# Scan rotation tables built on GpSimd during the second expert loop, window copies on VectorE, small mixing loads in SyncE's queue

## The chip, the cores and the metric

The kernel runs on one core of a Trainium2 chip. The metric is the device time of one execution in microseconds. The core's engines are TensorE (PE in the profile; its weight loads are PEld), VectorE (DVE), ScalarE (ACT), GpSimd (POOL) and SyncE (SP). Each runs its own list of instructions in order and meets the others only through semaphores. DMAs are issued from SyncE's and ScalarE's queues here and are carried by 16 DMA engines.

## The reference

One sequence of 256 tokens of 1024 channels goes through two blocks. The first block has two layers; the first mixes by pooling and the second by latent attention, and each ends with a mixture of 32 experts, of which every token uses two. The second block has one layer: a mixing layer, cross attention over a memory of 256 tokens, and a convolutional feed-forward part. All values are float32.

The part that the change touches most is the state-space branch (`_s5`) of the mixing layer. It has 32 groups of 64 complex states, each driven by 16 channels:

```
lam = lam_re + i*lam_im                    # per group and state
dt = exp(log_dt)                           # per group
a_bar = exp(lam * dt)
b_bar = (a_bar - 1) / lam * b
bu[t] = b_bar @ u[t]
s[t] = a_bar * s[t-1] + bu[t]              # complex, over 256 tokens
y[t] = real(c @ s[t]) + d * u[t]
```

`a_bar`, `b_bar` and the powers of the rotation `exp(i*th)`, th = lam_im*dt, depend on weights alone and on no token.

## The kernel before

**Stages.** The work runs in the order: pooling layer, experts of layer 0 (`moe(0)`), latent attention (`mla`), experts of layer 1 (`moe(1)`), mixing layer (`mix`), `cross`, `ffn`. Big weights come as slabs of 2 MB (4096 floats in each of 128 partitions) into a ring of six. SyncE issues them in one order, each when the slab six places before it has been used (`slabs_done`); so the loads of a later stage begin while an earlier one still computes. An expert takes three slabs (gate, up, down).

**The arena.** Nearly all other buffers are fixed places in one tile called `arena`, handed from stage to stage. `xs` holds the tokens sorted by expert; `hT` is the transposed input of a layer and is free during an expert loop, and `XN`, the normalised input, is free once the sorting products have read it.

**Pooling layer.** ScalarE (from L1261) normalises x, issues the four router loads of layer 0 (`router_loads`, L1233 to L1237), and writes the upper half of the transposed blocks (`hT_upper`, L1257) into `pl`; VectorE writes the lower half. TensorE multiplies them by `pool_w` (L640), beginning with the lower half. GpSimd scales the bias (L2138) and adds it to x (L2142). VectorE then adds TensorE's products to x (L1596, L1597: eight instructions), which frees layer 0's experts: TensorE transposes x (L612) and computes the router's logits (L655).

**Expert loop.** Before it, every token is routed and sorted; at its start, VectorE and ScalarE scale the sorted blocks (ScalarE at L1298). For each expert GpSimd reads the expert's first slot from memory into a register (`value_load`) and copies its window of 64 tokens out of `xs` into one of two `xw` buffers (L2165). TensorE multiplies the window by gate and up (L729), ScalarE applies silu (L1318), VectorE multiplies by the up part (`hids`, L1702), TensorE transposes (L745), ScalarE copies (L1325), TensorE multiplies by down (L772) and combines the experts' outputs with gate columns (L758) that VectorE makes one expert ahead of use (`window_gates`, L1714 and L1717). The steps are written with TensorE's gate and up products of the next expert ahead of the down product of the present one. A register loop runs over the experts between the first two and the last two.

**Mixing layer.** ScalarE issued twelve small loads during the routing of layer 1 (`s5_loads`): the state weights `s5_rows` and `ldt2`, `b_in`, four parts of `c_rows`, the input-gate weights `w_if` and their biases. The gain of the final norm of block one was issued in the expert loop (L1307). After the loop x is normalised twice. TensorE transposes the state rows (L971) and `c_rows` (L975) and computes the first slab, `u`. VectorE meanwhile computes the discretised states on tiles of 128x16 (L1870 to L1916): dt, the reduced angle `th`, `a_bar`, `b_bar` (`bbar`) and the powers `wre`, `wim` of the rotation for 1, 2, 4, ... 128 tokens.

The scan has eight steps q, each of four groups (two columns of 128 states). TensorE: one slab of the layer's input projection (L950 or L961), transposes of the padded b (L1057), the outputs of step q-1 (`outputs`, L996), the state inputs of step q (L1066), and for q from 3 a part of the other branch, the mLSTM (`gates_between`: L1005, L1011, L1019, L1028, L1035). GpSimd: masks b (`bpad`, L2205), builds the table of the rotation's 256 powers for the step's two columns by doubling, in eight levels of six instructions (L2216 to L2221), the four products of a level waiting for the level before, and masks c (`cblk`, L2229). VectorE: rotates the inputs with the table (L1994 to L2000), scans (L2004), rotates back (L2007 to L2014, `states`), and between the steps does convolutions (L1849, L1854), the skip term (L1928) and the mLSTM's exponents (L1947 to L1959) and products. ScalarE: evacuates slabs, copies the transposed b (L1454), and applies exponentials (L1485 to L1489) and gates (L1465). ScalarE's copy for step 5 stands behind the exponentials, which wait for VectorE's exponents of step 4.

The wait that ties VectorE to GpSimd in each step is this:

```
dve.wait_ge(s["e_ready"], q + 1)
dve.wait_ge(s["bu_mm"], q + 1)

dve.tensor_tensor(r1, u_re, e_re, ALU.mult)
```

## Time and profile before

| | |
|---|---|
| median of 3 runs | 1870.59 us (1866.02 to 1873.18) |
| profiled execution, its own time | 1867.0 us |
| its span in the profile | 1865.2 us |
| TensorE busy | 1657.4 us (89%) |
| VectorE busy | 447.4 us (24%) |
| ScalarE busy | 234.1 us (13%) |
| GpSimd busy | 234.7 us (13%) |
| DMA, mean over the span | 270 GB/s; 504 MB in all |
| TensorE's mean granted clock | 0.958 of full speed |

The profile shows one execution. A timeline row has the start and the duration in microseconds, the engine, the line, the operation, what it writes and reads, and in brackets how long the engine was idle before it and what ended that. A share of busy time is a mean over stages with different limits, so the stages have to be read one by one. Stages by time: pooling layer to 31 us, routing of layer 0 to 65, first expert loop to about 535, attention to 678, routing of layer 1 to 712, second expert loop to 1179, mixing layer to about 1430, the rest to the end.

### The profile page before, as it was taken

To read this page: it belongs to the slowest core of one execution; us is meant where nothing else is said; L and a number is where in the kernel's file an instruction comes from. 1 tells how busy PE (TensorE), PEld (TensorE's weight loads), DVE (VectorE), ACT (ScalarE), POOL (GpSimd) and SP (SyncE) were. 2 spreads that over 40 slices of the span, in tenths; PEclk is the share of its full clock that TensorE was granted. 3 is DMA by queue.
4 is the path that set the end of the run, shared out by engine and by line. 5 is a ranking of instruction groups with operands and counts; after the bars stand their busy time and mean duration, and the time that the engine had idled before them with its cause. 6 is when DMAs were issued, how large, how long until landed. Compare 5 with 4: busy or idle time off the path is not lost.

```text
span 1865.2 us, 22408 instructions
## 1 busy us (share of the span) xinstructions
PE 1657.4 (89%) x8961; PEld 1036.5 (56%) x8961; DVE 447.4 (24%) x964; ACT 234.1 (13%) x504; POOL 234.7 (13%) x495
## 2 busy tenths in 40 slices
PE   5899989999988678999989899798788898899998
PEld 4655444444446546554444444576677585488853
DVE  3211111111122231111111111475563102133411
ACT  2010000000021311000000000312111111100000
POOL 1000000000000000000000000099960000000000
PEclk8899999999998788999999999999899898999999
DMA  9499999999994035999999999832223343344410
GB/s 345 187 396 426 425 426 427 427 426 426 426 347 181 0 109 204 426 427 427 426 426 425 426 427 424 330 104 75 83 91 132 116 143 128 102 136 136 156 47 23
DMA packets 104421, 504.29 MB, mean 270 GB/s; under 512 B 16714, under 2 KB 42667, under 8 KB 71595
## 3 DMA queue, kind: packets, MB, share of 16 engines
q1 hardware_dynamic: 90551, 497.21, 66.0%
q10 hardware_dynamic: 13812, 6.31, 1.2%
q8 instruction: 37, 0.61, 0.1%
q14 instruction: 21, 0.17, 0.0%
HBM read 502.45 MB, written 1.05 MB: 270 GB/s over the span
## 4 chain that ended last, share of the span: by engine, by line
PE 50%; DMA 32%; POOL 9%; DVE 4%; issue 3%; ACT 2%; POOLq 0%; SPq 0%; DVEq 0%; ACTq 0%
DMA ring<-in_w_up 32%; PE PS L729 12%; PE PS L1183 8%; PE PS L1193 4%; PE PS L1130 3%; PE PS L961 3%; PE PS L772 3%; PE PS L674 2%; PE PS L1120 2%; PE PS L935 1%; PE PS L1111 1%; POOL arena L2220 1%; POOL XN L2219 1%; POOL XN L2216 1%; POOL arena L2221 1%
## 5 line engine op out<-in xcount | busy, mean ns | idle before, releaser
L729 PE MATMUL PS<-ring,arena 128*64 128x256 f32 x4096 | 470.1, 384 | 76.3 <-DMA ring<-in_w_up 53.5
L729 PEld LDWEIGHTS PS<-ring,arena 128*64 128x64 f32 x4096 | 296.7, 138 | 271.5 <-DMA ring<-in_w_up 73.9
L772 PE MATMUL PS<-ring,arena 128*64 128x512 f32 x1024 | 233.8, 598 | 1.1 <-ACT arena L1325 1.1
L1702 DVE TENSOR_TENSOR arena<-PS,arena 128x256 f32<-128x256 f32 x64 | 27.2, 425 | 802.5 <-ACT arena L1318 802.5
L2165 POOL COPY arena<-arena 128x512 f32 x64 | 60.5, 945 | 856.1 <-DVE arena L1702 796.6
L772 PEld LDWEIGHTS PS<-ring,arena 128*64 128x64 f32 x1024 | 68.2, 136 | 157.7 <-issue 157.7
L1183 PE MATMUL PS<-hT,ring 128*128 128x256 f32 x704 | 153.8, 382 | 1.0 <-issue 1.0
L1183 PEld LDWEIGHTS PS<-hT,ring 128*128 128x128 f32 x704 | 134.8, 192 | 20.0 <-issue 1.3
L758 PE MATMUL PS<-arena 64*128 64x512 f32 x512 | 127.2, 615 | 1.9 <-ACT arena L1334 1.9
L950 PE MATMUL PS<-hT,ring 128*128 128x256 f32 x448 | 100.3, 385 | 0.0
L950 PEld LDWEIGHTS PS<-hT,ring 128*128 128x128 f32 x448 | 86.4, 194 | 12.4 <-issue 0.5
L1325 ACT ACTIVATE arena<-PS 128x256 f32<-128x256 f32 x64 | 24.6, 384 | 521.1 <-PE PS L745 521.1
L1334 ACT ACTIVATE arena<-PS 128x512 f32<-128x512 f32 x64 | 38.2, 597 | 307.5 <-PE PS L772 304.1
L1193 PE MATMUL PS<-ring,arena 128*128 128x512 f32 x176 | 75.7, 592 | 0.0
L758 PEld LDWEIGHTS PS<-arena 64*128 64x128 f32 x512 | 44.1, 186 | 41.5 <-issue 30.2
L1193 PEld LDWEIGHTS PS<-ring,arena 128*128 128x128 f32 x176 | 33.4, 190 | 41.7 <-issue 41.4
L961 PE MATMUL PS<-ring,arena 128*128 128x512 f32 x128 | 55.4, 593 | 1.1 <-ACT arena L1530 1.1
L1849 DVE TENSOR_SCALAR arena<-PS,VT 128x256 f32<-128x256 f32 x52 | 24.9, 538 | 103.7 <-PE PS L1183 95.7
L1714 DVE SCALAR_TENSOR_TENSOR arena<-arena 128x512 f32<-128x512 f32 x64 | 47.5, 743 | 0.2
L1854 DVE SCALAR_TENSOR_TENSOR arena<-PS,VT,arena 128x255 f32<-128x255 f32 (+2 forms) x112 | 46.8, 476 | 1.2
L1717 DVE TENSOR_TENSOR arena<-arena 128x256 f32<-128x256 f32 x64 | 44.2, 691 | 2.2
L674 PE MATMUL PS<-arena,XN 128*128 128x256 f32 x128 | 36.6, 449 | 8.2 <-DVE arena L1666 8.2
(372 smaller groups left out, 1466.4 us busy)
## 6 DMA issues: line engine op xcount, KB each, us to landing
ring<-in_w_gate SPq DMA_DIRECT2D x64, 2048.0 KB, 25.5
ring<-in_w_up SPq DMA_DIRECT2D x64, 2048.0 KB, 25.6
ring<-in_w_down SPq DMA_DIRECT2D x64, 2048.0 KB, 24.6
ring<-in_f_w_up SPq DMA_DIRECT2D x22, 1024.0 KB, 6.6
ring<-in_w_in SPq DMA_DIRECT2D x9, 2048.0 KB, 20.5
ring<-in_f_w_down SPq DMA_DIRECT2D x5, 2048.0 KB, 7.7
ring<-in_x_wkv SPq DMA_DIRECT2D x4, 2048.0 KB, 8.0
ring<-in_wo SPq DMA_DIRECT2D x2, 2048.0 KB, 13.5
```

What stands on the lines that cost most here:

```text
L674: mm = pe.matmul(PS[:, 4 * half + c // 2, c % 2 * T:(c % 2 + 1) * T], XN_rows[:, t, c, :], sel[:, t, half * T:(half + 1) * T], start=(t == ...
L729: mm = pe.matmul(PS[half * WINDOW:(half + 1) * WINDOW, bank, m * half_f:(m + 1) * half_f], xw[bank][:, k, :], mat[:, k, half * half_f:(hal ...
L758: mm = pe.matmul(PS[:, 4 + 2 * t + half, :], buf[rows, t * P:(t + 1) * P], y2[rows, :], start=first, stop=last, skip_group_check=True)
L772: mm = pe.matmul(PS[half * WINDOW:(half + 1) * WINDOW, 3, :], hidT[:, w, k * WINDOW:(k + 1) * WINDOW], mat[:, k, half * 512:(half + 1) * 5 ...
L950: mm = pe.matmul(PS[:, b, f % 2 * T:(f % 2 + 1) * T], w[:, k, f * P:(f + 1) * P], x[:, k, :], start=(k == 0), stop=(k == kx - 1))
L961: mm = pe.matmul(PS[:, bank + t, :], x[:, k, t * P:(t + 1) * P], w[:, k, :], start=(k == 0), stop=(k == kx - 1))
L1130: mm = pe.matmul(PS[:, 2 * half + f // 2, f % 2 * T:(f % 2 + 1) * T], w[:, k, f * P:(f + 1) * P], x[:, k, :], start=(k == 0), stop=(k == K ...
L1183: mm = pe.matmul(PS[:, 2 * (j % 2) + h, f * T:(f + 1) * T], w[:, k, h, f * P:(f + 1) * P], hT[:, k, :], start=(k == 0), stop=(k == KD - 1))
L1193: mm = pe.matmul(PS[:, 4 + 2 * t + half, :], gF[:, c, t * P:(t + 1) * P], w[:, c - 4 * j, half * 512:(half + 1) * 512], start=(c == 0), st ...
L1714: dve.scalar_tensor_tensor(gates2, slots[:, 0, :], slot_of[:, w, bass.ds(linear(e, 1, 0), 1)], slots[:, 1, :], ALU.is_equal, ALU.mult).the ...
L1854: ins = dve.scalar_tensor_tensor(v, ps(f)[:, 0:T - back], taps[f][back], v, ALU.mult, ALU.add)
L2165: pool.tensor_copy(xw[(e[1] * windows + w) % 2], xs[:, :, bass.ds(start + w * WINDOW, WINDOW)])\
```

## The change

- **State matrices.** The three small state loads are issued by SyncE at the program's start. TensorE transposes the state rows in the pooling layer, after both halves of `pl` are written and before the pool products. ScalarE, after its upper blocks, issues the router loads, copies the transposed rows and takes dt; GpSimd, after adding the bias to x, computes what VectorE did before (`s5_discretise`, with the three subtractions of the angle now two instructions each). The reciprocal stays with VectorE, which waits for GpSimd's denominator in front of the pooling layer's output. TensorE waits for dt before it transposes x for layer 0.
- **Tables.** After the sorts of layer 1 GpSimd builds the rotation tables of all eight steps at once (`s5_tables`) into a 32 KB part of the arena (`E`), with `XN` as scratch, and then `bbar`. One signal, `e_ready`, tells that all is there.
- **Window copies.** VectorE makes them in both expert loops, right after `hids` and in front of `window_gates`, two experts ahead.
- **Loads.** `b_in` is loaded by ScalarE in the second expert loop, where the gain was. The gain, `c_rows`, `w_if` and the biases are issued by SyncE ahead of the mixing slabs, behind a wait for the last up slab.
- **Places.** The gate tables `slots`, `gates2` and `gates` move into `hT`, other buffers move within the arena; the gate outputs `gT` lie over `E`, so ScalarE waits for a step's states before it writes them.

```diff
@@ SyncE
+            for at, name in ((0, "s5_lam_re_2"), (32, "s5_lam_im_2")):
+                sp.dma_start(s5_rows[at:at + S5J, :], a[name][0].rearrange("(j g) p -> j (g p)", g=2)).then_inc(s["s5_loaded"], 16)
+            sp.dma_start(ldt2[64:64 + S5J, :], a["s5_log_dt_2"][0].rearrange("(j g) -> j g", g=2)).then_inc(s["s5_loaded"], 16)
             sp.wait_ge(s["vec2_loaded"], 16 * (len(VEC_PARTS) - FIRST_VECTORS))
...
+            def mix_loads():
+                sp.dma_start(gain, a["final_norm"].partition_broadcast(P)).then_inc(s["gain_loaded"], 16)
+                for ri, n in enumerate(("re", "im")):
+                    for d in range(2):
+                        sp.dma_start(c_rows[:, ri, :, d * S5P:(d + 1) * S5P],
+                                     a[f"s5_c_{n}_2"][0].rearrange("(c g) h p -> (g h) c p", c=S5C)).then_inc(s["mix_loaded"], 16)
+                sp.dma_start(w_if, w_in[:, IN_IF:IN_GATE].rearrange("(k p) n -> p k n", p=P)).then_inc(s["mix_loaded"], 16)
+                sp.dma_start(b_if[:, 0:MH], a["m_b_i_2"]).then_inc(s["mix_loaded"], 16)
+                sp.dma_start(b_if[:, MH:], a["m_b_f_2"]).then_inc(s["mix_loaded"], 16)
+            sp.wait_ge(s["slabs_done"], MIX0 - 2)
+            mix_loads()
@@ TensorE, pooling layer
+            pe.wait_ge(s["s5_loaded"], 16 * 3)
+            pe.wait_ge(s["s5_small"], 1)
+            hT_wait("pool")
+            for i in range(3):
+                r = slice(32 * i, 32 * i + S5J)
+                mm = pe.transpose(PS[:, 5 + i, 0:S5J], s5_rows[r, :], ident[r, r])
+            mm.then_inc(s["s5_turned"], 1)
@@ TensorE, moe
                 pe.wait_ge(s["x_ready"], MOE_X[layer])
+                if layer == 0:
+                    pe.wait_ge(s["s5_dt"], 1)
@@ ScalarE, pooling layer
             norm("pool")
-            router_loads(0)
             act.wait_ge(s["vec_ready"], 1)
             hT_upper("pool", ["pool_norm"], dsts=[pl])
+            router_loads(0)
+            act.wait_ge(s["s5_turned"], 1)
+            act.activation(lre, PS[:, 5, 0:S5J], ACT.Copy)
+            act.activation(lim, PS[:, 6, 0:S5J], ACT.Copy)
+            act.activation(dt, PS[:, 7, 0:S5J], ACT.Exp).then_inc(s["s5_dt"], 1)
+            act.wait_ge(s["s5_th"], 1)
+            act.activation(rad, xdt, ACT.Exp)
+            act.activation(sh, th, ACT.Sin, scale=0.5)
+            act.activation(s1, th, ACT.Sin).then_inc(s["s5_sin"], 1)
@@ ScalarE, moe
-                if layer:
-                    s5_loads()
...
-                        act.dma_start(gain, a["final_norm"].partition_broadcast(P)).then_inc(s["gain_loaded"], 16)
+                        s5_b_loads()
@@ ScalarE, mix
                 def gate(i):
                     j = i - MIX_SLABS.index("g0")
+                    act.wait_ge(s["states"], j + 1)
@@ VectorE, pooling layer
             dve.wait_ge(s["pool_biased"], TT)
+            dve.wait_ge(s["s5_th"], 2)
+            dve.reciprocal(den, den).then_inc(s["s5_small"], 1)
             for half in range(2):
@@ VectorE, experts
+                    def window(e, w):
+                        if isinstance(e[0], int) and linear(e, windows, w) == 2:
+                            sorted_wait(1)
+                        if isinstance(e[0], int) and linear(e, 1, 0) >= EXPERTS:
+                            return
+                        start = dve.value_load(starts[0:1, bass.ds(linear(e, 1, 0), 1)], min_val=0, max_val=SLOTS)
+                        dve.tensor_copy(xw[(e[1] * windows + w) % 2], xs[:, :, bass.ds(start + w * WINDOW, WINDOW)])\
+                           .then_inc(g["window"], 1)
...
                                 hids(next_expert(e), w)
+                                window(*after(next_expert(e), w))
                             window_gates(e, w)
@@ VectorE, mix
-                    dve.wait_ge(s["e_ready"], q + 1)
+                    if q == 0:
+                        dve.wait_ge(s["e_ready"], 1)
                     dve.wait_ge(s["bu_mm"], q + 1)
@@ GpSimd
+            def s5_discretise():
+                pool.wait_ge(s["s5_dt"], 1)
+                pool.tensor_tensor(xdt, lre, dt, ALU.mult)
+                step(pool.tensor_tensor(th, lim, dt, ALU.mult))
+                step(pool.tensor_scalar(kq, th, 1.0 / (2 * math.pi), None, ALU.mult))
+                step(pool.tensor_scalar(kq, kq, 12582912.0, None, ALU.add))
+                step(pool.tensor_scalar(kq, kq, 12582912.0, None, ALU.subtract))
+                for part in (6.28125, 0.0019350051879882812, 3.019915981956753e-07):
+                    step(pool.tensor_scalar(ta, kq, part, None, ALU.mult))
+                    step(pool.tensor_tensor(th, th, ta, ALU.subtract))
+                pool.tensor_scalar(th, th, 3.1415925, -3.1415925, ALU.min, ALU.max).then_inc(s["s5_th"], 1)
+                pool.tensor_tensor(ta, lre, lre, ALU.mult)
+                step(pool.tensor_tensor(tb, lim, lim, ALU.mult))
+                pool.tensor_tensor(den, ta, tb, ALU.add).then_inc(s["s5_th"], 1)
...
+            def s5_tables():
+                pool.wait_ge(s["sorted_mm"], KD // 2 * 4)
+                pool.wait_ge(s["slots_spread"], 2)
...
+                for k in range(8):
+                    n = 1 << k
+                    m = min(S5J // 2, 256 // n)
...
+                    for q in range(0, S5J // 2, m):
...
+                        pool.tensor_tensor(tmp[0], e_re[:, :, :, 0:n], g_re, ALU.mult)
+                        pool.tensor_tensor(tmp[1], e_im[:, :, :, 0:n], g_im, ALU.mult)
+                        pool.tensor_tensor(tmp[2], e_re[:, :, :, 0:n], g_im, ALU.mult)
+                        step(pool.tensor_tensor(tmp[3], e_im[:, :, :, 0:n], g_re, ALU.mult))
+                        pool.tensor_tensor(e_re[:, :, :, n:2 * n], tmp[0], tmp[1], ALU.subtract)
+                        step(pool.tensor_tensor(e_im[:, :, :, n:2 * n], tmp[2], tmp[3], ALU.add))
...
+            s5_discretise()
+            moe(0)
+            moe(1)
+            s5_tables()
             mix()
```

## Rows read from the trace of the kernel before

**Rows 1.** The page, the chain that ended last, by engine.
```profile
PE 50%; DMA 32%; POOL 9%; DVE 4%; issue 3%; ACT 2%; POOLq 0%; SPq 0%; DVEq 0%; ACTq 0%
```

**Rows 2.** Windows: stretch, length, busy us (instructions), granted clock, DMA share, GB/s.
```profile
820.00:1170.00 350.00, 317.94 (x2162) 156.45 (x2158) 43.84 (x74) 30.33 (x73) 21.53 (x22) 1.00 1.01 426
1210.00:1400.00 190.00, 166.54 (x699) 132.02 (x699) 116.75 (x206) 36.37 (x56) 163.24 (x420) 0.93 0.26 92
1284.00:1286.00 2.00, 2.00 (x6) 1.64 (x5) 0.00 (x0) 1.01 (x1) 1.82 (x9) 0.50 0.92 371
```

**Rows 3.** Waits in the scan, 1210 to 1390 us.
```profile
DVE XN L1994 <- POOL arena L2221: 39.5, 4, 11.3
```

**Rows 4.** Timeline of VectorE in scan steps 2, 4 and 7.
```profile
1271.32 0.69 DVE L1994 TENSOR_TENSOR XN<-PS,arena 128x512 f32<-128x512 f32 x1 [11.26 <-POOL arena L2221]
...
1316.03 0.69 DVE L1994 TENSOR_TENSOR XN<-PS,arena 128x512 f32<-128x512 f32 x1 [9.57 <-POOL arena L2221]
...
1332.48 1.66 DVE L1959 TENSOR_TENSOR arena<-arena 128x512 f32<-128x512 f32 x2
...
1382.97 0.69 DVE L1994 TENSOR_TENSOR XN<-PS,arena 128x512 f32<-128x512 f32 x1 [8.30 <-POOL arena L2221]
```

**Rows 5.** Timeline of TensorE in scan steps 3 to 5.
```profile
1283.41 3.40 PE L996 MATMUL PS<-arena 128*128 128x256 f32 x8 [4.16 <-DVE arena L1928]
...
1307.97 1.88 PE L1011 MATMUL PS<-arena,const 128*128 128x512 f32 x4
...
1338.84 3.78 PE L1066 MATMUL PS<-arena 128*128 128x256 f32 x8 [7.82 <-ACT arena L1454]
```

**Rows 6.** Timeline of GpSimd, levels 0 and 7 of step 0's table.
```profile
1213.15 0.20 POOL L2219 TENSOR_TENSOR XN<-arena,mtmp 128x2 f32<-128x2 f32 x1
1213.42 0.20 POOL L2220 TENSOR_TENSOR arena<-XN 128x2 f32<-128x2 f32 x1
...
1226.36 0.72 POOL L2221 TENSOR_TENSOR arena<-XN 128x256 f32<-128x256 f32 x1
```

**Rows 7.** Timeline of VectorE and TensorE in the second expert loop.
```profile
1135.55 0.42 DVE L1702 TENSOR_TENSOR arena<-PS,arena 128x256 f32<-128x256 f32 x1 [12.99 <-ACT arena L1318]
...
1136.66 0.72 DVE L1717 TENSOR_TENSOR arena<-arena 128x256 f32<-128x256 f32 x1
...
1140.49 3.67 PE L729 MATMUL PS<-ring,arena 128*64 128x256 f32 x32 [0.26 <-DMA ring<-in_w_gate]
...
1151.34 0.42 DVE L1717 TENSOR_TENSOR arena<-arena 128x256 f32<-128x256 f32 x1
```

**Rows 8.** Timeline of ScalarE and GpSimd at the second loop's start.
```profile
707.22 0.84 ACT L1298 ACTIVATE arena<-PS,ffn_gain 128x256 f32<-128x256 f32 x2 [1.02 <-PE PS L674]
...
709.83 1.28 POOL L2165 COPY arena<-arena 128x512 f32 x2 [29.76 <-issue]
```

**Rows 9.** Windows, columns as in rows 2.
```profile
687.00:688.00 1.00, 0.00 (x0) 0.00 (x0) 0.90 (x8) 0.00 (x0) 0.00 (x0) 0.50 1.06 109
52.00:62.00 10.00, 7.65 (x28) 6.90 (x27) 3.20 (x13) 2.77 (x5) 0.00 (x0) 0.89 0.01 2
```

**Rows 10.** Timeline of TensorE at the start of the mixing layer.
```profile
1187.01 3.67 PE L612 MATMUL PS<-const,XN 128*128 128x128 f32 x16 [8.31 <-DVE XN L1569]
...
1192.76 13.98 PE L950 MATMUL PS<-hT,ring 128*128 128x256 f32 x64
```

**Rows 11.** Timeline of the pooling layer, all engines.
```profile
12.76 4.24 ACTq L1236 DMA_DIRECT2D arena<-in_router_group_b  x1
...
22.34 0.84 ACT L1257 ACTIVATE arena<-PS,VT 128x256 f32<-128x256 f32 x2 [0.41 <-PE PS L631]
...
25.03 0.69 DVE L1596 TENSOR_TENSOR arena<-PS,arena 128x512 f32<-128x512 f32 x1 [4.85 <-PE PS L640]
...
30.44 0.69 DVE L1597 TENSOR_TENSOR X<-X,arena 128x512 f32<-128x512 f32 x1
31.19 1.97 PE L612 MATMUL PS<-const,X 128*128 128x128 f32 x16 [1.98 <-DVE X L1597]
```

More of the change, by code:

```diff
@@ L484, in program @@
         mxe, wdif, wst, m_prev = st_(92, MH), st_(96, MH), st_(100, MH), st_(104, MH)
-        mx, bm, em_, dn, hss, hrm = (ar(19464 + 8 * i, TT, MH) for i in range(6))
-        iw = ar(19512, MH)
+        mx, bm, em_, dn, hss, hrm = (ar(19468 + 8 * i, TT, MH) for i in range(6))
+        iw = st_(108, MH)
         memt = ar(0, TT, D)
@@ L2136, in _, with step @@
         def _(pool):
[L2137 to L2139 removed]
+            steps = [0]
+            def step(ins):
+                steps[0] += 1
+                ins.then_inc(s["pool_step"], 1)
+                pool.wait_ge(s["pool_step"], steps[0])
+            pool.wait_ge(s["pool_loaded"], 16 * 3)
+            step(pool.tensor_tensor(pool_b, pool_b, pool_scale, ALU.mult))
+            pool.wait_ge(s["s5_loaded"], 16 * 3)
+            pool.tensor_copy(s5_rows[64:64 + S5J, :].rearrange("j (g p) -> j g p", g=2),
+                             ldt2[64:64 + S5J, :, None].to_broadcast([S5J, 2, S5P])).then_inc(s["s5_small"], 1)
+            pool.wait_ge(s["s5_small"], 1)
             pool.wait_ge(s["norm_xn"], TT)
@@ L2142, in _ @@
                 pool.tensor_tensor(X[:, t, :], X[:, t, :], pool_b, ALU.add).then_inc(s["pool_biased"], 1)
+            def s5_discretise():
[12 more added lines that the diff above has]
+                pool.tensor_tensor(den, ta, tb, ALU.add).then_inc(s["s5_th"], 1)
+                pool.wait_ge(s["s5_sin"], 1)
+                step(pool.tensor_tensor(cmn, sh, sh, ALU.mult))
+                step(pool.tensor_scalar(cmn, cmn, -2.0, None, ALU.mult))
+                pool.tensor_scalar(c1, cmn, 1.0, None, ALU.add)
+                pool.tensor_tensor(ta, rad, cmn, ALU.mult)
+                pool.tensor_scalar(tb, rad, 1.0, None, ALU.subtract)
+                step(pool.tensor_tensor(aim, rad, s1, ALU.mult))
+                step(pool.tensor_tensor(are, ta, tb, ALU.add))
+                pool.wait_ge(s["s5_small"], 2)
+                for o, x, y, op in ((cfre, are, aim, ALU.add), (cfim, aim, are, ALU.subtract)):
+                    pool.tensor_tensor(ta, x, lre, ALU.mult)
+                    step(pool.tensor_tensor(tb, y, lim, ALU.mult))
+                    step(pool.tensor_tensor(ta, ta, tb, op))
+                    step(pool.tensor_tensor(o, ta, den, ALU.mult))
+                pool.tensor_copy(wre[:, 0, :], c1)
+                step(pool.tensor_copy(wim[:, 0, :], s1))
+                for k in range(7):
+                    pool.tensor_tensor(ta, wre[:, k, :], wre[:, k, :], ALU.mult)
+                    pool.tensor_tensor(tb, wim[:, k, :], wim[:, k, :], ALU.mult)
+                    step(pool.tensor_tensor(kq, wre[:, k, :], wim[:, k, :], ALU.mult))
+                    pool.tensor_tensor(wim[:, k + 1, :], kq, kq, ALU.add)
+                    step(pool.tensor_tensor(wre[:, k + 1, :], ta, tb, ALU.subtract))
@@ L2156, in experts @@
-                def experts(windows):
-                    g = loop[layer]
-                    def step(e, last):
-                        start = pool.value_load(starts[0:1, bass.ds(linear(e, 1, 0), 1)], min_val=0, max_val=SLOTS)
-                        for w in range(windows):
-                            if isinstance(e[0], int) and linear(e, windows, w) == 2:
-                                sorted_wait(1)
-                            wait(pool, g["hidden"], linear(e, windows, w - 1))
-                            pool.tensor_copy(xw[(e[1] * windows + w) % 2], xs[:, :, bass.ds(start + w * WINDOW, WINDOW)])\
-                                .then_inc(g["window"], 1)
-                    expert_steps(pool, step)
@@ L2190, in mix @@
                 pool.wait_ge(s["stage_loaded"], 32)
-                pool.wait_ge(s["s5_bbar"], 1)
-                pool.wait_ge(s["ct_act"], 1)
-                pool.wait_ge(s["if_mm"], 1)
-                for e in turns:
-                    pool.memset(e[:, 0, :, 0:1], 1.0)
-                    ins = pool.memset(e[:, 1, :, 0:1], 0.0)
-                step(ins)
                 for q in range(S5J // 2):
```

212 lines of the change are left out of this document (67 added, 145 removed).

## The prediction, on record before the changed kernel ran

> **What bounds the kernel now.** I read the chain that ended last first, by engine [rows 1]: TensorE holds 50% of it, the DMA 32% and GpSimd 9%. GpSimd's 9% is the only part of it that this change aims at. The windows say where each limit lies [rows 2]. In the second expert loop (820 to 1170 us) the DMA engines are full, share 1.01 at 426 GB/s, and GpSimd is busy 21.5 of 350 us, so its time there is free; in the scan of the mixing layer (1210 to 1400 us) the DMA share is 0.26, TensorE is busy 166.5 of 190 us and GpSimd 163.2. So the expert loops run at the pace of the loads, and the scan runs between TensorE and GpSimd. The waits of the scan name the link [rows 3]: VectorE waited 39.5 us, four times, for GpSimd's last table instruction (L2221). TensorE's own two longest waits there are 4.16 and 7.82 us [rows 5]. What can be won is what TensorE lost and what the last step adds, not the 39.5 us and not GpSimd's 163 us.
>
> **The scan, step by step.** TensorE needs about 17.6 us for a scan step that waits for nothing (one slab 13.9, then transposes, outputs and state inputs, 3.7). I replay the trace with the tables ready.
> - Step 2 (counted from 0): VectorE was done with step 1 at 1260.1 and could start when TensorE's inputs end, 1264.9; it started at 1271.3, after 11.26 us of idle [rows 4]. With tables it is 6.4 us earlier, its states are ready at 1275.8, and TensorE's 4.16 us wait before the outputs [rows 5] goes, together with the 1.5 us that these outputs took longer at the low clock after that wait (3.40 us; 1.89 us elsewhere). The next slab starts at 1283.0 in place of 1288.7: 5.7 us won.
> - Step 4: TensorE's inputs now end at 1300.7, so VectorE starts there and not at 1316.0 [rows 4]. Its states take 10.75 us, then the skip term and the exponents 7.5 us (in the trace to 1334.1): 1319.0. From there ScalarE's exponentials, gates and copy took 4.7 us until TensorE's inputs of step 5 (1334.1 to 1338.8 in rows 4 and 5): 1323.7 in place of 1338.8. So 15.1 us are won by here. But a wait stays: TensorE is ready at 1318.5 and still waits 5.2 us for that chain. This is what is late next, and no table helps it.
> - Steps 5 and 6 run as before, shifted. In step 7 VectorE started at 1382.97, 1.9 us after TensorE's inputs, on GpSimd [rows 4]: that goes too, so the last states come 17.1 us earlier.
> - Against this: TensorE now waits some 4 us for these last states, and the wait of 4.16 us before 1283.4 left it at the lower of its two levels, 1.2 GHz (granted 0.50 from 1284 to 1286 us [rows 2], and 3.40 us for the outputs). I take 1.5 us of the 17.1 back. Scan: -15.6 us; bounds -12 (clock lost here and in step 5) and -17.5.
> - VectorE's small instructions on the state matrices (1192 to 1206 us) lay under TensorE's first slab [rows 10] and are worth nothing; nor is ScalarE's new wait for the states before the gates, since gate slab j waits for step j, done four steps before. The three small transposes that TensorE loses there cost 0.24 us.
>
> **The tables in the loop.** GpSimd builds them in 12 batches of six instructions, seven of 512 columns and five of fewer. An instruction of 256 columns took up to 0.72 us [rows 6]; twice that for 512 columns gives at most 1.44 x 42 = 60 us, and the smaller ones at most 0.72 x 30 = 22 us, so 82 us as a bound from above. It starts after the sorts, near 740 us, and is wanted at 1178 us: hidden five times over. The kernel's cover for it is the whole loop.
>
> **The window copies go to VectorE.** Each expert: a register load and a copy of 128x512. VectorE's copy has no row; its 128x1024 scaling takes 0.75 us, so 0.4 us. In the loop the product (L1702) ends at 1135.97 and TensorE starts the next gate slab at 1140.49 [rows 7]; GpSimd's copy took 0.98 us of these 4.5. VectorE has the same 4.5 us for load and copy, since the gate products behind them are used only one expert later. At the loop's start GpSimd began its first copy 1.8 us after ScalarE's last sorted block [rows 8], two register loads and a branch included, so a load takes 0.9 us at most. I take 0, bounds 0 and +4 us for both loop entries together. The gate sum (L1717) took 0.72 us beside GpSimd's copy and 0.42 us without one [rows 7]: each of the two engines slows the other, and during the table build VectorE's 2 us of work an expert may become 3, inside a 14.75 us step. The Trainium skill, GPSIMD Engine Reference, section "1. Specifications", says that GpSimd shares its SBUF interfaces with VectorE and contends with VectorE instructions that have two SBUF inputs or use both ports; it thus speaks against putting the copies beside the tables, and the trace agrees with it, at 0.3 us that nobody waits for.
>
> **The loads.** The DMA paces the loop, so each microsecond added within it counts once. The loads of c, the small input-gate weights and the biases leave ScalarE's queue; before, they ran while the ring was full and the engines idle, so removing them wins nothing. The two loads of b (2 x 2048 pieces of 64 B) move into the loop, in the place of the final norm's gain (512 KB, 1.2 us at 427 GB/s). Between 682 and 690 us, in which such pieces went, the engines were full (share 1.06 from 687 to 688) at 101 to 207 GB/s [rows 9]: about 1.44 MB in 7.3 us of engine time, of which 1.5 us was slabs, so 5.8 us for about 7200 pieces of 32 to 256 B, 13 ns each on one of 16 engines. That makes b 3.3 us, less 1.2: +2.1 us; bounds 0 (gaps in the first steps) and +6 (twice the price). The Trainium skill, DMA: Bandwidth & Descriptors, section "Specifications", puts the size for full rate at 512 B or more and thus speaks against it; counted by bytes alone b would be 0.6 us, and the trace agrees with the page. In SyncE's queue the eight small loads now stand before the mixing slabs, behind a wait for the last up slab (1163.8 us). The last down slab lands near 1170; some 4 us of small loads and 5.4 us of a slab at 387 GB/s bring the first mixing slab at about 1180, and TensorE wants it at 1192.8 [rows 10]: 13 us of cover. The gain lands near 1173 and is wanted at 1181.8, 8 us. Everything queued behind (the further slabs) has a longer lead. Cost 0; without cover it would be 1 for 1.
>
> **The start.** Here the change adds a chain before the first layer's output. ScalarE now issues the four router loads after its upper blocks (they end at 23.2), and only then reads the transposed state rows. The third of these issues alone held ScalarE 4.24 us [rows 11], the four 5.7 us at 12 us and 5.2 us in the loop: ScalarE is free at 28.2. Two copies, a table load of 1.28 us and an Exp: 30.1. Then GpSimd's chain to the denominator, 11 dependent steps at 0.28 us (0.27 from L2219 to L2220 [rows 6]) and four undependent at 0.15: 34.0. VectorE waits for it, takes the reciprocal (0.25 us), and only then writes the layer's output, which it began at 25.03 [rows 11]. Eight instructions, 5.45 us: x ready at 39.7 in place of 31.13, +8.6 us. TensorE also waits for both halves before its pool products (22.14 to about 24), which is covered by this. It is then idle from about 31 to 39.7; after such a gap at 1179 to 1187 us its 16 transposes took 3.67 us, against 1.97 us here [rows 10, 11], so +1.4 us; the logits, half of which ran at the low clock, may give 0.5 back. Start: +9.5 us. The ring of six slabs is full at about 50 us and the DMA idle (share 0.01 from 52 to 62 [rows 9]) until the loop begins, so the loop and every load in it move by the same 9.5 us. Bounds: +5 if the issues don't hold ScalarE, +14 if a GpSimd step on 16 columns takes 0.65 us, as instructions of few columns beside a busy VectorE did.
>
> **Sum.** +9.5 (start) +2.1 (b) +0 (windows) -15.6 (scan) = -4.0 us on the profiled execution's 1867.0 us: 1863.0. The median of the runs is 3.6 us above that execution, so 1866.6, said as 1867.
>
> **The rivals.**
> - No loss at the start: the router loads issue fast, or the chain hides under TensorE's 7 us of pool products. For it: the issue took 0.39 to 0.60 us for two of the four. Against it: the wait stands in VectorE's own order before the output, and the held issue is in the trace twice. Then -13.5 us: 1857. Chance 0.20.
> - The window copy becomes a wait in each step, the case that ends slower. It decides once load and copy on VectorE pass 4.5 us, or once steps get longer than the 14.75 us of the loads; every 0.3 us beyond costs 0.3 x 60 = 18 us, so with my other terms +14: 1885. Against it: GpSimd's 1.8 us for two loads and a branch. Chance 0.10.
> - The start costs more: GpSimd's steps at twice or three times 0.28 us: +5 to +8 us more, 1872 to 1875. For it: few-column instructions of 0.45 to 0.68 us in the scan. Against: those had a busy VectorE beside them. Chance 0.15, a third of it over the bound when joined with dearer b loads.
> - The change doesn't do its work: the scan stays with VectorE and ScalarE at step 4 and wins 5.7 us only: +6, 1876. Chance 0.05.
> - The forecast: 0.50.
>
> Half a per cent is 9.4 us, about what a measurement of this kernel can tell from no change. Faster: the first rival and a tail of the forecast, 0.25. Slower: the second and the tail of the third, 0.15. Same: 0.60. The range runs from the low bounds (+5 +0 -17.5, 1858) and the first rival to the high ones (+14 +6 -12 +2, 1881): 1857 to 1880; what it leaves out is mostly the second rival.
>
> **What would show it.** Right: VectorE's first pool output near 34 us and x ready near 40; the expert steps at 14.75 us still; the first mixing slab without a wait; VectorE's state work starting within 0.1 us of TensorE's inputs in all eight steps; one TensorE wait of about 5 us in step 5. Wrong, if VectorE's first output starts by 28 us, if TensorE shows waits for a VectorE copy in the loop, or if the scan from its first slab to the last outputs is not 15 to 17 us shorter.

## The result and the profile after

The changed kernel took 1889.27 us (median of 4 runs, 1886.73 to 1890.52), the kernel before 1871.12 us beside it (4 runs, 1866.02 to 1873.18): ratio 1.0094, 95% interval 1.0068 to 1.0120. So it is slower, outside the range of 1857 to 1880. The profiled execution took 1889.9 us with a span of 1887.9, against 1867.0 and 1865.2 before: 22.7 us of span.

I went along the span and compared the start of the same instruction in both traces, after minus before. Each difference holds what has been lost up to there. A "turn" is TensorE's transposing of x ahead of a layer; the "logits" are the router's.

| place | after, us | minus before, us | predicted |
|---|---|---|---|
| TensorE turns the first layer's output | 60.87 | +29.7 | +8.6 |
| VectorE has the first logits | 72.57 | +33.5 | +9.5 |
| first gate slab of loop 1 | 98.81 | +33.7 | +9.5 |
| layer-1 turn | 713.74 | +35.5 | +9.5 |
| first gate slab of loop 2 | 750.06 | +37.5 | +9.5 |
| first mixing slab | 1232.61 | +39.9 | +11.6 |
| inputs of scan step 5 | 1362.70 | +23.9 | -3.5 |
| slab behind the last outputs of the scan | 1419.41 | +22.7 | -4.0 |

The scan gives back 17.1 us, 1.5 more than I gave it; the start takes three and a half times what I gave it. This is the timeline of the start, all engines:

```profile
18.47 0.35 SPq L540 DMA_DIRECT2D ring<-in_w_gate  x1
...
21.31 0.47 SPq L540 DMA_DIRECT2D ring<-in_w_gate  x1
...
21.69 0.38 ACTq L1254 DMA_DIRECT2D arena<-in_router_group_w  x1
...
22.11 0.68 ACTq L1255 DMA_DIRECT2D arena<-in_router_expert_w  x1
...
22.82 25.71 ACTq L1256 DMA_DIRECT2D arena<-in_router_group_b  x1
22.83 7.17 PE L664 MATMUL PS<-arena 128*128 128x256 f32 x32
48.55 0.48 ACTq L1257 DMA_DIRECT2D arena<-in_router_expert_b  x1
49.08 0.18 ACT L1289 ACTIVATE mtmp<-PS 128x16 f32<-128x16 f32 x1 [26.55 <-issue]
...
50.90 0.22 POOL L2148 TENSOR_TENSOR mtmp<-mtmp 128x16 f32<-128x16 f32 x1 [26.77 <-ACT mtmp L1291]
...
55.31 0.25 DVE L1608 RECIPROCAL mtmp<-mtmp 128x16 f32<-128x16 f32 x1 [35.37 <-POOL mtmp L2160]
...
60.13 0.69 DVE L1614 TENSOR_TENSOR X<-X,arena 128x512 f32<-128x512 f32 x1
...
60.87 3.67 PE L629 MATMUL PS<-const,X 128*128 128x128 f32 x16 [30.86 <-DVE X L1614]
...
65.52 7.01 PE L681 MATMUL PS<-arena,hT 128*128 128x36 f32 x32 [0.97 <-issue]
```

The third router load's issue holds ScalarE for 25.71 us (4.24 us in rows 11). The releaser of the copy behind it reads "issue": no semaphore, the engine itself was held. Everything after it is what I had worked out, only later: the exponential, 4.3 us of GpSimd's chain (I had 3.9), then 5.5 us for the reciprocal and the outputs. SyncE issued six slabs between 18.5 and 21.3 us. The last of them landed at 51.8 us; the hold ends 3.3 us before that. The windows of the same kernel (columns as in rows 2) and its DMA issues (KB each, us from issue to landing):

```profile
22.00:49.00 27.00, 7.34 (x35) 6.17 (x35) 0.00 (x0) 0.52 (x2) 2.12 (x1) 0.69 1.01 419
49.00:62.00 13.00, 1.13 (x6) 1.13 (x7) 5.37 (x9) 7.47 (x15) 8.14 (x30) 0.50 0.18 48
```

```profile
arena<-in_router_expert_w ACTq DMA_DIRECT2D x1, 128.0 KB, 29.8
arena<-in_router_group_w ACTq DMA_DIRECT2D x1, 16.0 KB, 29.9
arena<-in_router_group_b ACTq DMA_DIRECT2D x1, 2.0 KB, 29.3
arena<-in_router_expert_b ACTq DMA_DIRECT2D x1, 16.0 KB, 4.1
```

So there are two losses, one on the other: ScalarE is held until 48.6 us, and the router weights land at 51.9 us (22.11 + 29.8), when the logits of the kernel before had long been run (34.4). The windows show the third: TensorE, which had nothing to do from 30 to 60.9 us, has a granted clock of 0.50 (1.2 GHz) from 49 to 62 us, and the logits take 7.01 us in place of 4.63.

The scan after, TensorE's timeline at step 5 and at the last outputs:

```profile
1362.70 3.02 PE L1086 MATMUL PS<-arena 128*128 128x256 f32 x8 [4.29 <-ACT arena L1467]
...
1414.74 3.65 PE L1017 MATMUL PS<-arena 128*128 128x256 f32 x8 [4.29 <-DVE arena L2004]
```

The wait of step 5 is 4.29 us (I had left it 5.2), and a new one of 4.29 us stands before the last outputs (I had "some 4"), which then ran 3.65 us at the low clock against 1.99. VectorE waits for no GpSimd table any more.

### The profile page after: what moved, and what is told of

The parts are those of the page before. It is cut to its first block, busy times and chain, and to the rows that moved or that the text cites. A ratio compares the mean times of both kernels' runs of the same rounds, so it can differ in the third digit from the quotient of the medians.

```text
span 1887.9 us, 22005 instructions
## 1 busy us (share of the span) xinstructions
PE 1659.1 (88%) x8961; PEld 1037.6 (55%) x8961; DVE 452.4 (24%) x962; ACT 235.9 (12%) x507; POOL 113.5 (6%) x191
## 3 DMA queue, kind: packets, MB, share of 16 engines
q1 hardware_dynamic: 93947, 498.30, 65.5%
## 4 chain that ended last, share of the span: by engine, by line
PE 55%; DMA 33%; DVE 5%; issue 3%; ACT 2%; ACTq 1%; POOL 0%; DVEq 0%; SPq 0%
DMA ring<-in_w_up 32%; PE PS L755 11%; PE PS L1203 8%; PE PS L976 5%; PE PS L987 4%; PE PS L1213 4%; PE PS L1150 3%; PE PS L798 2%; PE PS L700 2%; PE PS L1140 2%; PE PS L961 1%; PE PS L1131 1%; ACTq L1256 1%; PE PS L784 1%; PE PS L629 1%
## 5 line engine op out<-in xcount | busy, mean ns | idle before, releaser
L784 PE MATMUL PS<-arena,hT 64*128 64x512 f32 x512 | 127.2, 615 | 1.9 <-ACT arena L1352 1.9
L784 PEld LDWEIGHTS PS<-arena,hT 64*128 64x128 f32 x512 | 44.0, 186 | 41.5 <-issue 30.2
L1750 DVE SCALAR_TENSOR_TENSOR hT<-hT,arena 128x512 f32<-128x512 f32 x64 | 51.1, 798 | 0.2
L1266 ACT ACTIVATE XN<-X 128x1024 f32<-128x1024 f32 x18 | 18.9, 1050 | 185.8 <-DVE X L2069 85.0
```

Source lines behind the costliest of these rows:

```text
L784: mm = pe.matmul(PS[:, 4 + 2 * t + half, :], buf[rows, t * P:(t + 1) * P], y2[rows, :], start=first, stop=last, skip_group_check=True)
L1750: dve.scalar_tensor_tensor(gates2, slots[:, 0, :], slot_of[:, w, bass.ds(linear(e, 1, 0), 1)], slots[:, 1, :], ALU.is_equal, ALU.mult).the ...
```

## The experiments

Theory: the issue of the third router load is held because SyncE's slabs are ahead of it, and the 30 us follow from that. "Held" means that the issuing instruction itself lasts that long; "landing" is when the data are in. Rivals: GpSimd's chain with VectorE's new wait costs them wherever the loads stand; or the loads are dear themselves.

**1. Router loads early again.** Of the changed kernel, only the place of the loads:

```diff
             norm("pool")
+            router_loads(0)
             act.wait_ge(s["vec_ready"], 1)
             hT_upper("pool", ["pool_norm"], dsts=[pl])
-            router_loads(0)
```

> The changed kernel with ScalarE's four router loads issued before its upper blocks again, as in the kernel before. Theory (the third router load's issue is held 25.7 us because SyncE's six slab loads, queued at 18.5 to 21.3 us, go first): all four are issued by about 17.5 us, the exponential of the step sizes starts near 25 us, GpSimd's denominator is done 4.3 us after it, near 30, and x is ready near 35.5 us in place of 60.8 (31.1 before). Start +4 to +8 us, scan -17, b loads +2.7: 1859 to 1866 us, 23 to 30 us less than the changed kernel. Rival (GpSimd's chain and VectorE's new wait cost the 30 us wherever the loads stand): x ready stays near 60 us and the time near 1889.

Measured: 1862.14 us (8 runs), ratio to the kernel before 0.9949 (0.9932 to 0.9967). Its timeline:

```profile
12.72 4.49 ACTq L1256 DMA_DIRECT2D arena<-in_router_group_b  x1
...
28.65 0.25 DVE L1608 RECIPROCAL mtmp<-mtmp 128x16 f32<-128x16 f32 x1 [9.76 <-POOL mtmp L2160]
...
34.22 3.34 PE L629 MATMUL PS<-const,X 128*128 128x128 f32 x16 [5.25 <-DVE X L1614]
...
38.74 5.42 PE L681 MATMUL PS<-arena,hT 128*128 128x36 f32 x32 [1.19 <-issue]
```

The same chain and the same wait of VectorE are there, and cost 3.0 us up to the turn and 5.1 us up to the end of the logits, with the clock's part. The place of the loads is worth 27 us.

**2. The kernel before with the loads late**, the reverse of that edit and nothing else.

> The kernel before with one edit: ScalarE issues the four router loads after its upper blocks, as in the changed kernel; nothing else of the change. Theory: the third issue is held as in the changed kernel, from 22.8 to about 48.5 us. x is ready at 31.1 us as before, since nothing ahead of it waits for ScalarE, but ScalarE's half of the first layer's norm and upper blocks and the router rows themselves come only then, so the logits start near 52 us in place of 34.4: +16 to +20 us, 1883 to 1890. Rival (the hold comes from something else that the change added, the three small state loads in SyncE's queue or GpSimd): the issue takes 4 to 5 us and the time is 1867 to 1872.

Measured: 1891.33 us (4 runs), ratio 1.0108 (1.0084 to 1.0132), a little over the 1883 to 1890 expected. The output was ready as before, the turn started at 30.98 us, and the third issue and TensorE's first logits show what came next:

```profile
23.27 25.39 ACTq L1236 DMA_DIRECT2D arena<-in_router_group_b  x1
...
53.69 7.01 PE L655 MATMUL PS<-arena,hT 128*128 128x36 f32 x32 [20.74 <-ACT hT L1257]
```

So one moved line, without any of the table work, makes the kernel 20 us slower: what it hits here is ScalarE's half of the next layer's norm.

**3 and 4. The slabs held back, all or three of them**, with the loads late as in the changed kernel:

```diff
+            sp.wait_ge(s["row_loaded"], 64)      # 3: ahead of the first slab
             experts(0, MOE0)
...
+                        if n0 + j == 3:          # 4: ahead of the fourth
+                            sp.wait_ge(s["row_loaded"], 64)
                         one(n0 + j, *expert_slab(j))
```

> The changed kernel with one wait added: SyncE waits for the four router loads to land before it issues the first expert slab. Theory (the slabs in the other queue hold the issue): the third issue takes about 4 us, ScalarE is free near 28, x is ready at 38 to 41 us; the slabs start near 28 in place of 18.5 us and are all in near 58, ahead of the first gate slab at about 75. Start +9 to +13 us: 1864 to 1870. Rival (the pieces of the router loads cost 26 us of themselves, whoever else is in the queues): the issue stays at 20 us or more, the slabs start only near 50 and the time is 1889 or more.

> The changed kernel, with SyncE issuing three expert slabs and then waiting for the four router loads before the other three. If the issue is held until the bytes queued ahead of it have gone, half the slabs hold it half as long: 6 MB from 18.5 us at 427 GB/s, so until 33 to 35 us; x ready near 46 us, time 1872 to 1878. If the hold is all or nothing (any slab ahead makes it as long), x is ready near 60 and the time 1889 or, with the other slabs coming later still, more; if only a queue filled by the later three slabs holds it, x is ready near 40 and the time 1864 to 1870.

Measured: 1862.27 us (7 runs), ratio 0.9948 (0.9930 to 0.9966), with none ahead, and 1873.93 us (10 runs), ratio 1.0009 (0.9995 to 1.0024), no difference from the kernel before, with three. The third issue in the one and in the other:

```profile
22.55 0.60 ACTq L1257 DMA_DIRECT2D arena<-in_router_group_b  x1
```

```profile
23.19 9.96 ACTq L1258 DMA_DIRECT2D arena<-in_router_group_b  x1
```

0, 6 and 12 MB of slabs ahead give 0.60, 9.96 and 25.71 us. The hold ends at 33.2 and 48.5 us. An estimate from 6 and 12 MB at 427 GB/s, counted from 18.5 us, gives 33 and 48 us; the last slabs themselves landed 3.2 and 3.3 us after the hold, at 36.3 and 51.8. The weights landed after 2.7, 14.3 and 29.8 us. So the length of the hold goes with what the other queue has under way, and the loads by themselves cost 0.60 us. Whether the bytes or the number of the slabs count isn't parted, since all slabs have 2 MB.

I had expected about 4 us for the third issue of experiment 3, and it took 0.60. This throws light on the 4.24 us of the kernel before: there the DMA engines were full (share 1.09 from 12 to 17 us) with other loads, and in experiment 3 they weren't (share 0.34 from 20 to 24 us). So the 4.24 us fit a hold of the same kind; they are not a fixed price of the issue.

**5 and 6. What does the holding?** The late loads in another order (5: biases first, then the two weight loads), and only the two weight loads late (6):

```diff
+                act.dma_start(rb[:, 0:GROUPS], ...)      # 5: these two first
+                act.dma_start(rb[:, GROUPS:], ...)
                 act.dma_start(rw[:, :, 0:GROUPS], ...)
                 act.dma_start(rw[:, :, GROUPS:], ...)
-                act.dma_start(rb[:, 0:GROUPS], ...)
-                act.dma_start(rb[:, GROUPS:], ...)
```

> The changed kernel, with the late router loads in another order: the two bias loads first, then the group and expert weights (1024 pieces each). In the changed kernel the two weight loads were issued in 0.4 and 0.7 us and the third issue held. If the number of loads outstanding holds it, the third, now the group weights, is held until 48 us. If their pieces do (1024 and 1024 fill it), three go at once and the fourth, the expert weights, is held. If it is something in the bias load itself, the first is held. ScalarE is free near 48 us in each case, and the time is 1885 to 1893.

> The changed kernel with the two small bias loads issued early, where the kernel before had all four, and only the two weight loads late. This parts the hold of ScalarE from the late landing of the weights. Theory: nothing is behind the two weight loads, so ScalarE isn't held and x is ready near 35 us in place of 60.8; but the weights land only with the slabs, near 52 us, and the logits wait for them, so 12 to 14 us come back of the 30: 1874 to 1879 us. If the hold is the whole cost, the logits start near 39 us and the time is 1860 to 1865.

Measured: 1880.12 us in a single run, so without an interval (5), and 1874.53 us in 10 runs, ratio 1.0026 (1.0010 to 1.0041) (6). With the biases first no issue was held:

```profile
21.86 0.34 ACTq L1254 DMA_DIRECT2D arena<-in_router_group_b  x1
22.24 0.47 ACTq L1255 DMA_DIRECT2D arena<-in_router_expert_b  x1
22.74 0.51 ACTq L1256 DMA_DIRECT2D arena<-in_router_group_w  x1
...
23.28 0.66 ACTq L1257 DMA_DIRECT2D arena<-in_router_expert_w  x1
```

This was in none of my three cases, and the time was under the 1885 to 1893 expected. The same four loads, behind the same slabs, hold ScalarE only if something is issued behind both weight loads of 1024 pieces each (8 for each of 128 partitions). Where exactly the limit lies is left open. The landings differ too:

```profile
arena<-in_router_expert_w ACTq DMA_DIRECT2D x1, 128.0 KB, 30.2
arena<-in_router_group_b ACTq DMA_DIRECT2D x1, 2.0 KB, 10.9
arena<-in_router_expert_b ACTq DMA_DIRECT2D x1, 16.0 KB, 15.5
arena<-in_router_group_w ACTq DMA_DIRECT2D x1, 16.0 KB, 30.3
```

The biases, first in their queue, landed in the middle of the slabs, and only the weights about with their end. That the late landing is a cost of its own was as expected: in both, the output was turned at 35.8 and 34.7 us, and the logits waited for the weights. TensorE in 6:

```profile
51.94 7.01 PE L681 MATMUL PS<-arena,hT 128*128 128x36 f32 x32 [13.53 <-DMA arena<-in_router_expert_w]
```

So of the 31 us by which the logits of the changed kernel start late (65.5 against 34.4), 17.5 belong to the landing, which alone would stop them until 51.9, and the hold adds 13.6. The time of 6 is as expected (1874 to 1879).

**7. VectorE's wait behind the pool output**, added to experiment 1:

```diff
-            dve.wait_ge(s["s5_th"], 2)
-            dve.reciprocal(den, den).then_inc(s["s5_small"], 1)
             for half in range(2):
                 ...
+            dve.wait_ge(s["s5_th"], 2)
+            dve.reciprocal(den, den).then_inc(s["s5_small"], 1)
```

> The kernel with the router loads first (1862.1 us), and VectorE's wait for the denominator with its reciprocal moved behind the pool output instead of ahead of it. With the loads first, x was ready 3.0 us later than in the kernel before, the turn took 3.34 us (1.97 before) and the logits 5.42 (4.64 before), 5.1 us in all until VectorE had the logits. Theory (all of this comes from VectorE's place in the order): x is ready at 31.1 to 31.5 us again, the clock holds, and 3 to 5 us go: 1857 to 1859. Rival (GpSimd's chain beside VectorE and ScalarE's table loads cost as much wherever the wait stands): x is ready at 32 or later and the time stays at 1862.

Measured: 1859.44 us (6 runs), ratio 0.9939 (0.9920 to 0.9958). A middle result: the turn started at 32.34 us and not at 31.1. About 1.0 us of that is not the moved wait's: the pool products began at 23.13 us and at 22.14 in the kernel before, since in the changed kernel they also wait for ScalarE's half of the blocks (written by 22.8 us here) and for the three transposes. The rest of the loss is ScalarE's: it was still behind its own wait for GpSimd's angle, its squares of the norm began at 32.87 (29.84 before), and the logits at 37.25. The wait had only changed engines.

**8. All state arithmetic off the start.** ScalarE makes three plain copies before the turn; the rest runs in the first routing:

```diff
-            act.activation(dt, PS[:, 7, 0:S5J], ACT.Exp).then_inc(s["s5_dt"], 1)
-            act.wait_ge(s["s5_th"], 1)
-            act.activation(rad, xdt, ACT.Exp)        # and the two sines
+            act.activation(dt, PS[:, 7, 0:S5J], ACT.Copy).then_inc(s["s5_dt"], 1)
...
                 hT_upper(name, ["ffn_norm"], KD * layer)
+                if layer == 0:
+                    act.wait_ge(s["s5_dt"], 1)
+                    act.activation(dt, dt, ACT.Exp).then_inc(s["s5_dt"], 1)
+                    act.wait_ge(s["s5_th"], 1)
+                    act.activation(rad, xdt, ACT.Exp)    # and the two sines
```

VectorE's reciprocal stands at the end of its routing, GpSimd's chain behind its memset of the first layer.

> The same, with all state arithmetic off the start: before the first layer's turn ScalarE only makes three plain copies; the exponentials, sines and GpSimd's chain run while ScalarE waits for the routing of the first layer, and VectorE takes the reciprocal at the end of its routing. Theory: the start is that of the kernel before, within 1 us; GpSimd's small instructions beside VectorE's routing cost up to 1 us; scan -17, second loop +2.7: 1855 to 1859 us, ratio 0.991 to 0.994. Rival (GpSimd's chain slows VectorE's routing, or ScalarE comes late to the exponentials of the routing): the first gate slab starts over 2 us later than in the kernel before and the time stays at 1860 or more.

Measured: 1854.74 us (6 runs), ratio 0.9923 (0.9898 to 0.9947). The turn started at 31.34 us (31.19 before), the first gate slab at 65.73 (65.12).

**9. The loads of b in the second routing**, on top of experiment 8:

```diff
                 if layer == 0:
                     ...
+                if layer:
+                    s5_b_loads()

                 act.wait_ge(s["route_max"], q + 1)
...
                         router_loads(1)
-                    else:
-                        s5_b_loads()
```

> The kernel with the state arithmetic off the start, and ScalarE's two loads of b moved from the second expert loop to the second layer's routing, where the DMA engines are idle. Theory (within the loop the DMA paces, so b costs its own DMA time there, and nothing while the ring is full): the second loop gets 2 to 3.3 us shorter and the time 1852 to 1856. Rival (the 2.7 us that the second loop got longer come from VectorE's copies and work beside the table build, not from the loads): no difference from the kernel with the arithmetic off the start.

Measured: 1851.91 us (6 runs), ratio 0.9909 (0.9885 to 0.9934): the fastest version, 19 us under the kernel before and 37 under the changed one. The runs alone don't part it from experiment 8; the traces do. From the second loop's first gate slab to the first mixing slab it is 480.2 us in the kernel before, 482.5 in the changed one, 482.3 in experiment 8 and 480.0 here. Not all of this lies in the loop. Up to the mixing layer's turn it is 474.4, 477.1, 475.9 and 474.5 us; the rest of the difference between experiments 8 and 9 comes right behind the loop, where TensorE's turn and its transposes of `c_rows` ran slower in the one trace:

```profile
1189.57 3.68 PE L629 MATMUL PS<-const,XN 128*128 128x128 f32 x16 [8.34 <-DVE XN L1587]
1194.22 1.94 PE L996 MATMUL PS<-const,arena 128*128 128x128 f32 x8 [0.97 <-issue]
```

```profile
1187.95 3.45 PE L629 MATMUL PS<-const,XN 128*128 128x128 f32 x16 [8.34 <-DVE XN L1587]
1192.48 1.07 PE L996 MATMUL PS<-const,arena 128*128 128x128 f32 x8 [1.08 <-issue]
```

So the loads of b cost 1.4 us inside the loop by this pair; the loop of the changed kernel was 2.7 us longer than that of the kernel before.

**10 and 11. The cover of the window copies**, on top of experiment 9: three and ten more register loads of the same start ahead of each copy.

```diff
-                        start = dve.value_load(...)
+                        for _ in range(4):           # 11 in the last experiment
+                            start = dve.value_load(...)
```

> The kernel with b loaded early, and in front of each of VectorE's window copies three more register loads of the same start, to use up the cover of the copy. A load takes 0.5 us, so each copy ends some 1.5 us later, at 1193.2 in place of 1191.7 us in the step whose next gate slab starts at 1195.46. If the copy has 3.7 us of cover, the steps stay at 14.75 us and the time at that of the kernel without them, plus 2 to 3 us at the two loop entries, where the copies stand on the path. If the copies are a wait already, 1.5 us times 62 steps come on top: 1940 or more.

> As the kernel with three more register loads ahead of each window copy (they took 0.57 us each, and 2.35 us stood between the product and the copy in place of 0.5), now with ten more: 6.3 us of loads and 0.43 of copy, against the 4.1 us from the end of VectorE's product to the next gate slab. The prediction's rival said that the copy decides once load and copy pass 4.5 us. From a gate slab's start to the product's end VectorE and TensorE need 10.2 us, of which TensorE's wait of 1.2 us for the up slab would go: 9.0 + 6.7 = 15.7 us a step in place of 14.75, +55 us over 58 steps of two loops, and some 12 us at the entries: 1915 to 1930 us, and TensorE's waits for the DMA turn into waits for the copy. If the cover is larger than I read, 1865 to 1875.

Measured, one run each and so without an interval: 1860.84 and 2052.46 us. With three more I had expected 1854 to 1855 us. With them the loop has no wait for a copy but one of 1.1 us at its entry, and the loss is in the entries and in a low clock of the second logits (6.25 us against 3.74). The entries cost some 6 us in place of the 2 to 3 expected. With ten more each step waits:

```profile
314.38 8.80 PE L755 MATMUL PS<-ring,arena 128*64 128x256 f32 x64 [2.77 <-DVE arena L1736]
...
331.87 8.59 PE L755 MATMUL PS<-ring,arena 128*64 128x256 f32 x64 [2.76 <-DVE arena L1736]
```

I had expected 63 to 78 us (1915 to 1930) and it was 200: a step takes 15.8 to 17.5 us. The wait was as I had it or a little longer, but behind most of these waits (all but one of the seven between 290 and 415 us) the two slabs took 8.5 to 8.8 us in place of 7.1, with a granted clock of 0.92 from 150 to 450 us (1.00 without the loads).

## Why the prediction was wrong

**The start: the failed step.** "The third of these issues alone held ScalarE 4.24 us [rows 11], the four 5.7 us at 12 us and 5.2 us in the loop: ScalarE is free at 28.2." The step that failed is this cost: it was carried over from loads that stood ahead of SyncE's slabs, and in their new place they stand behind 12 MB of them. The one issue measured 25.7 us in place of 4.24, and ScalarE was free at 49.0 us in place of 28.2. I had looked at where the loads stand in ScalarE's order and at how long they took, and not at what the other queue has under way at that time, though my text gave both numbers (the issues after 23.2 us, the ring full at about 50). The upper bound of +14 priced a slower GpSimd and left the hold at 5 us. Nor did I ask when the weights would land: this alone would have made the start +17.5 us and more (experiment 6: turn at 34.7, logits at 51.94). Experiments 1 to 4 show the cause in both directions and by dose. Why it is the load behind two of 1024 pieces that is held (experiment 5) stays open.

The Trainium skill, DMA: Bandwidth & Descriptors, section "Issuing engines are not separate DMA queues", says that DMAs started by different engines "will ultimately run on the same 16 DMA engines and interleave with each other". The traces agree that they share; but 16 KB took 29.9 us to land, so little came of the interleaving for them; the biases of experiment 5, first in their queue, landed after 10.9 and 15.5 us, so the queues do take turns. Section "Queues, rings and completion order" has the DMA engines change between queues only after a whole packet of pieces, some 9 to 17. By that a turn of ScalarE's queue, with its small pieces, waits for a turn of SyncE's, whose pieces are large, and the weights come in only about as the slabs end. This fits the landings of 14.3 and 29.8 us and those of the biases, but it is only argued here: no run changed the size of the slabs' pieces.

**The rest of the start was right in kind.** In experiment 1, where the hold is away, the chain of the exponential, GpSimd and VectorE costs 3.0 us up to the turn and 5.1 us up to the end of the logits. My +8.6 and +9.5 had 5.0 us of issues in them (23.2 to 28.2), so 3.6 and 4.5 us without them. I had a GpSimd step at 0.28 us, and it took 0.33 us. The turn at the low clock took 3.67 us, as taken. That the logits would give 0.5 us back was wrong: they took 2.4 us more.

**The scan was right.** 17.1 us won net between the first scan slab and the slab behind the last outputs, -15.6 predicted; 16.0 by step 5 (15.1 predicted); the waits that stay were named and sized within 1 us. This rests on one trace of each kernel; no experiment took the tables out alone.

**The loads of b: right in the net, and in part by luck.** +2.7 us up to the mixing layer's turn and +2.4 up to its first slab, +2.1 predicted. But I had 3.3 us for b and 1.2 us back for the gain; by experiments 8 and 9 b cost 1.4 us, and without the gain the loop was no shorter (474.5 against 474.4 us). Counted by bytes, b for the gain would have won 0.6 us, and that is not what happened. The Trainium skill, DMA: Bandwidth & Descriptors, section "Specifications", puts full rate at 512 B or more, and these traces agree in direction: the pieces of 64 B took over twice the 0.6 us of their bytes.

**The window copies: right.** Register load and copy took 0.5 and 0.43 us, the steps stayed at 14.75 us, and the entries cost 0.5 and 0.3 us (TensorE's wait there is 5.98 and 5.70 us, 5.47 and 5.41 before). In the rival on them the price was too low: where a copy does become a wait, the clock is lost too, 3.2 us a step and not 0.95 (experiment 11). Its point of decision, 4.5 us, lies between the two tried: 2.4 + 0.4 us did not decide and 6.6 + 0.4 did.

**The tables: right.** 512 columns took 1.09 to 1.33 us on GpSimd (bound 1.44), all were ready at 847 us, and VectorE first read them at 1270. VectorE's gate product beside them took 1.53 us (0.74 alone) and its window copy 1.40 us (0.43 alone), more than I gave it, and nobody waited for that.

**Left open:** 1.8 us between the first gate slab and the second layer's turn and 2.4 us in that layer's logits, which ran 6.22 us in place of 3.78 at the low clock. Experiment 1 has the same code and 3.78 us there, so the 2.4 us are the clock's and not the code's; the 1.8 us fit it, with a granted clock of 0.94 over the last 34 us before that turn against 0.98 in experiment 1. What decides where it falls was not found.

## What to carry to other kernels

A load is priced by its place among all queues, not only by its place on its engine: write down the bytes that every other queue has under way when it is issued, and divide by the rate; that is roughly when it lands (48 us by this sum, 51.9 measured; the loads first in their own queue came sooner), and roughly when the engine may be let go. A price of an issue read from a trace holds only for the traffic that it was read in. Small loads that the next stage needs go ahead of bulk transfers or on an engine that has nothing behind them, and a wait that is moved should be followed through every engine, since it comes out again on the next one. An order in which a side computation touches a critical engine only with plain copies, and does the rest in a stage where that engine idles, kept the whole gain of this change (0.9909 of the time before).

## What the runs showed of the hardware

An issue on one engine can be held nearly as long as another engine's transfers run: 25.7 us behind 12 MB, 10.0 behind 6 MB, 0.6 behind none. With 6 and with 12 MB the hold ended some 3 us before the last of these slabs landed. At the start it struck only the load issued behind two of 1024 pieces each. In an order that ends with these two, all four were issued in 0.7 us or less; the two landed just as late, after 30 us, and the biases ahead of them after 10.9 and 15.5 us. The second load of b, behind 2048 pieces, held ScalarE 4.25 us in the full loop and 3.93 us in the routing (experiment 9). And a wait of 2.8 us in each step of TensorE's otherwise full loop brought its granted clock from 1.00 to 0.92 over 300 us, and the matmuls behind most waits took 1.3 to 1.7 us longer, about half as much again as the wait itself.
